# First normalisation of a two-block layer kernel in two halves of 512 tokens

## The reference, cut to what matters

```python
def rms_norm(x, w):
    xf = x.astype(jnp.float32)
    y = xf * lax.rsqrt(jnp.mean(xf * xf, axis=-1, keepdims=True) + EPS)
    return (y * w.astype(jnp.float32)).astype(x.dtype)

def hybrid_block(x, norm1_w, w_in, ...):
    h = rms_norm(x, norm1_w)
    proj = h @ w_in            # q, k, v of the attention come first here
...
def s5_ssm(u, a_re, a_im, log_dt, ...):
    lam = lax.complex(a_re, a_im)
    dt = jnp.exp(log_dt)[:, None]
    a_bar = jnp.exp(lam * dt)
    zoh = (a_bar - 1.0) / lam
```

## Time and profile before

| | |
|---|---|
| median of 3 runs | 3429.97 us (3427.22 to 3436.2) |
| profiled execution, its time | 3430.34 us |
| its span (first to last instruction) | 3428.4 us |
| mean granted TensorE clock | 0.983 |
| TensorE busy | 96% of the span |
| VectorE, ScalarE, POOL busy | 43%, 30%, 38% |
| first product pair starts | 37.26 us |
| block 2 starts | 64.49 us |

### The profile page before, as it was taken

One profiled execution on the slowest core, in us unless ns is written; L12 is line 12 of the kernel. 1 busy time (PEld: TensorE's weight loads), 2 busy tenths in 40 slices (PEclk: granted clock), 3 DMA queues, 4 the chain that ended last, 5 costly groups with the idle time before them and its releaser, 6 DMA issues. The chain is left out here.

```text
span 3428.4 us, 51094 instructions
## 1 busy us (share of the span) xinstructions
PE 3283.3 (96%) x20680; PEld 2707.5 (79%) x20680; DVE 1479.0 (43%) x2368; ACT 1012.7 (30%) x1728; POOL 1315.8 (38%) x1102
## 2 busy tenths in 40 slices
PE   6999999999898999999999999999899999999999
PEld 5888888777787887887788888888688877777877
DVE  4333333263656555457633333333382144444343
ACT  3444444432443434301211111111222044432221
POOL 4222222252424242335434333344434355554543
PEclk9999999999999999999899999999899999999999
DMA  2100000103112011214111111111331111111122
GB/s 105 36 32 32 31 32 32 38 22 112 37 32 56 20 49 28 87 54 156 51 57 49 43 49 49 49 49 49 120 87 47 48 46 42 52 46 46 58 86 80
DMA packets 104198, 188.06 MB, mean 55 GB/s; under 512 B 32328, under 2 KB 64712, under 8 KB 101328
## 3 DMA queue, kind: packets, MB, share of 16 engines
q1 hardware_dynamic: 91536, 179.19, 16.0%
q10 hardware_dynamic: 12480, 6.29, 0.6%
HBM read 158.33 MB, written 27.12 MB: 54 GB/s over the span
## 5 line engine op out<-in xcount | busy, mean ns | idle before, releaser
L303 PE MATMUL DP<-XH,WH 128*128 128x512 f32 x2592 | 832.6, 402 | 18.3 <-POOL WL L251 18.3
L249 POOL CAST WH<-WRAW 128x1024 fp32r<-128x1024 f32 (+2 forms) x258 | 269.2, 1043 | 1484.2 <-issue 900.5
L303 PE MATMUL DP<-XL,WH 128*128 128x512 f32 x2592 | 804.7, 392 | 0.0
L303 PE MATMUL DP<-XH,WL 128*128 128x512 f32 x2592 | 803.5, 391 | 0.0
L251 POOL TENSOR_TENSOR WL<-WRAW,WH 128x1024 fp32r<-128x1024 f32 (+2 forms) x258 | 588.5, 2281 | 20.8
L303 PEld LDWEIGHTS DP<-XH,WL 128*128 128x128 f32 x2592 | 488.7, 189 | 105.6
L303 PEld LDWEIGHTS DP<-XL,WH 128*128 128x128 f32 x2592 | 488.8, 189 | 105.0
L303 PEld LDWEIGHTS DP<-XH,WH 128*128 128x128 f32 x2592 | 467.6, 189 | 120.0 <-issue 24.3
L870 DVE SCALAR_TENSOR_TENSOR SS<-B,RQ,SBI 128x256 f32<-128x256 f32 (+2 forms) x192 | 74.3, 428 | 314.8 <-PE B L569 314.8
L379 DVE TENSOR_TENSOR XR<-XR,B 128x1024 f32<-128x1024 f32 x88 | 106.6, 1220 | 90.7 <-PE B L359 88.4
L2320 DVE SCALAR_TENSOR_TENSOR TG<-DP,COL,TG 128x1023 f32<-128x1023 f32 x44 | 56.4, 1283 | 199.8 <-ACT TG L2308 197.0
(11 more groups left out here) (480 smaller groups left out, 5176.3 us busy)
## 6 DMA issues: line engine op xcount, KB each, us to landing
WRAW<-in_w_up SPq DMA_DIRECT2D x44, 512.0 KB, 3.5
WRAW<-in_w_attn SPq DMA_DIRECT2D x36, 512.0 KB, 3.5
WRAW<-in_w_down SPq DMA_DIRECT2D x22, 512.0 KB, 3.5
XR<-in_x SPq DMA_DIRECT2D x8, 1024.0 KB, 8.0
WRAW<-in_w_dn SPq DMA_DIRECT2D x16, 512.0 KB, 3.8
aa_dram<-AA ACTq DMA_DIRECT2D x12, 512.0 KB, 3.3
YY<-yy_dram SPq DMA_DIRECT2D x12, 512.0 KB, 4.1
WRAW<-in_w_lrux SPq DMA_DIRECT2D x10, 512.0 KB, 3.4
```

Of the source, the lines that this page charges most:

```text
L249: pool.tensor_copy(WH[b.slot][:, 0:b.kt, :], WRAW[b.slot][:, 0:b.kt, :]).then_inc(w_hi, 1)
L303: mm = pe.matmul(DP[b.slot][:, half * H:half * H + H], w[b.slot][:, k, :], x[:, k, half * H:half * H + H], start=one, stop=end)
```

## The change

It leaves the arithmetic as it is and splits the first normalisation, its loads and its first product pair by tokens, 0 to 511 and 512 to 1023. The other three normalisations run through the same helpers, rewritten so that they take a range of tokens, and are as before.

- SP loads the first half of x in four transfers of 0.5 MB, then constants and the two weight blocks, then the second half in three transfers, which count on `mx_out`, `ks_out` and `w1_out` (later waits on these are raised by 16). SP no longer waits for `pr_sm`.
- ScalarE squares the first half, loads the table of the root (`norm_warm`), takes the first root, and then works on both halves in an order written out below. Behind both it waits for `pr_sm` and issues the two small transfers to DRAM itself, ahead of `attn_act`, which begins with `take_q`.
- VectorE does only the angle part ahead of the normalisation; the 21 chained operations and `pr_sm` come behind the last scaling of the second half.
- TensorE's `product2_halves` takes the first half for all k of both blocks, with the second half's sums ahead of k = 4 and its transposes ahead of k = 6; then the second half for k = 0 to 3 of both blocks, then k = 4 to 7 of block 0, then of block 1.
- `NTL`, `SQ`, `RS`, `XH` and `XL` keep their places; each half uses its own columns of them.

```diff
+        def scale_one(dve, c, k, src, w):
+
+            if k == 0:
+                dve.wait_ge(rs_sum, c.root + 2)
+            if k >= 2:
+                dve.wait_ge(nt_used, c.nt + k - 1)
+            elif c.nt0:
+                dve.wait_ge(nt_used, c.nt0)
+            dve.scalar_tensor_tensor(out=NTL[k % 2][:, c.tok], in0=src[:, k, c.tok], scalar=col(w, k), in1=c.spread,
+                                     op0=ALU.mult, op1=ALU.mult).then_inc(nt_ready, 1)
+        def hi_one(act, c, k):
+
+            act.wait_ge(nt_ready, c.nt + k + 1)
+            act.activation(XH[:, k, c.tok], NTL[k % 2][:, c.tok], ACT.Copy).then_inc(xh_ready, 1)
...
+        def product2_halves(pe, blocks, hi, lo, cs, within=None):
+
+            for b in blocks:
+                pe.wait_ge(w_split, b.n + 1)
+                pe.wait_ge(psum_free[b.slot], b.loads - 1)
+            for half, c in enumerate(cs):
+                t = slice(half * H, half * H + H)
+                steps = [(b, k) for k in range(KD if half == 0 else 4) for b in blocks]
+                if half:
+                    steps += [(b, k) for b in blocks for k in range(4, KD)]
+                for b, k in steps:
+                    if b is blocks[0]:
+                        if half == 0 and within:
+                            within(k)
+                        pe.wait_ge(xh_ready, c.nt + k + 1)
+                        pe.wait_ge(nt_used, c.nt + k + 1)
+                    for w, x, one, end in ((WH, hi, k == 0, False), (WH, lo, False, False), (WL, hi, False, k == KD - 1)):
+                        mm = pe.matmul(DP[b.slot][:, t], w[b.slot][:, k, :], x[:, k, t], start=one, stop=end)
+                    if half and k == KD - 1:
+                        mm.then_inc(mm_done, 1)
...
@@ SP
-                    sp.dma_start(XR[:, 2 * i:2 * i + 2, :], a["x"][:, 2 * i:2 * i + 2, :]).then_inc(mx_in[i], 16)
+                    sp.dma_start(XR[:, 2 * i:2 * i + 2, 0:H], a["x"][:, 2 * i:2 * i + 2, 0:H]).then_inc(mx_in[i], 16)
                 sp.dma_start(CON[:, :], a["cst"]).then_inc(con_in, 16)
                 sp.dma_start(COL[:, :], a["cols"]).then_inc(con_in, 16)
                 for i in range(2):
                     load(sp, Block("attn", 0, i), a["w_attn"])
+                for k, n, landed in ((0, 2, mx_out), (2, 2, ks_out), (4, 4, w1_out)):
+                    sp.dma_start(XR[:, k:k + n, H:T], a["x"][:, k:k + n, H:T]).then_inc(landed, 16)
...
@@ ScalarE, behind prep_act
+                def square1(i, k):
+                    act.wait_ge((mx_out, ks_out, w1_out, w1_out)[k // 2] if i else mx_in[k // 2], 16)
+                    norm_square(act, c1[i], k, XR[:, k, c1[i].tok])
                 for k in range(KD):
-                    act.wait_ge(mx_in[k // 2], 16)
-                    norm_square(act, c1, k, XR[:, k, :])
-                norm_sqrt(act, c1)
-                norm_hi(act, c1)
+                    square1(0, k)
+                norm_warm(act)
+                norm_sqrt(act, c1[0])
+                hi_one(act, c1[0], 0)
+                hi_one(act, c1[0], 1)
+                for k in range(5):
+                    square1(1, k)
+                for k in range(5, KD):
+                    hi_one(act, c1[0], k - 3)
+                    square1(1, k)
+                hi_one(act, c1[0], 5)
+                hi_one(act, c1[0], 6)
+                norm_sqrt(act, c1[1])
+                hi_one(act, c1[0], 7)
+                norm_hi(act, c1[1])
+                act.wait_ge(pr_sm, 1)
+                act.dma_start(r8_dram, SM[:, 8, :]).then_inc(pr_out, 16)
+                act.dma_start(sk_dram, SM[:, 13:27, :].rearrange("p r t -> p (r t)")).then_inc(pr_out, 16)
                 attn_act(act)
...
@@ VectorE
+                prep_angle(dve)
+                for k in range(1, KD):
+                    norm_add(dve, c1[0], k)
+                norm_inverse(dve, c1[0])
+                dve.wait_ge(con_in, 32)
+                def scale1(i, k):
+                    scale_one(dve, c1[i], k, XR, "norm1")
+                scale1(0, 0)
+                scale1(0, 1)
+                for k in range(1, 5):
+                    norm_add(dve, c1[1], k)
+                for k in range(5, KD):
+                    scale1(0, k - 3)
+                    norm_add(dve, c1[1], k)
+                scale1(0, 5)
+                scale1(0, 6)
+                norm_inverse(dve, c1[1])
+                for k in range(7, KD):
+                    scale1(0, k)
+                for k in range(KD):
+                    scale1(1, k)
                 prep_dve(dve)
-                for k in range(1, KD):
-                    norm_add(dve, c1, k)
-                norm_inverse(dve, c1)
-                dve.wait_ge(con_in, 32)
-                norm_scale(dve, c1, XR, "norm1")
```

More of the change, by code:

```diff
@@ L394, in program, with __init__ @@
         class NormCount:
-            def __init__(self, i):
-                self.sq, self.ss, self.nt = KD * i, i, KD * i
-                self.acc, self.root = 7 * i, 2 * i
+            def __init__(self, sq, acc, nt, root, tokens=(0, KD), sums=None, spread=None, nt0=None):
+                self.sq, self.acc, self.nt, self.root, self.ss = sq, acc, nt, root, root // 2
+                self.tiles = range(*tokens)
+                self.tok = slice(P * tokens[0], P * tokens[1])
+                self.sums = B67[:, 0:16] if sums is None else sums
+                self.spread = B45[:, self.tok] if spread is None else spread
+                self.nt0 = nt if nt0 is None else nt0
@@ L400, in norm_square, with counts @@
+        def counts(n):
+            return [n + i + 1 for i in range(KD)]
         def norm_square(act, c, k, src):
             if k >= 2:
-                act.wait_ge(sq_used, c.acc + max(k - 2, 1))
-            act.activation(SQ[k % 2][:, :], src, ACT.Square).then_inc(sq_ready, 1)
+                act.wait_ge(sq_used, c.acc[max(k - 2, 1)])
+            act.activation(SQ[k % 2][:, c.tok], src, ACT.Square).then_inc(sq_ready, 1)
         def norm_add(dve, c, k):
-            dve.wait_ge(sq_ready, c.sq + k + 1)
+            dve.wait_ge(sq_ready, c.sq[k])
@@ L408, in norm_add @@
             if k > 1:
-                dve.wait_ge(sq_used, c.acc + k - 1)
-            dve.tensor_tensor(RS[:, :], (RS if k > 1 else SQ[0])[:, :], SQ[k % 2][:, :], ALU.add).then_inc(sq_used, 1)
+                dve.wait_ge(sq_used, c.acc[k - 1])
+            dve.tensor_tensor(RS[:, c.tok], (RS if k > 1 else SQ[0])[:, c.tok], SQ[k % 2][:, c.tok], ALU.add).then_inc(
+                sq_used, 1)
         def norm_sum(pe, c):
-            pe.wait_ge(sq_used, c.acc + 7)
-            for t in range(KD):
-                mm = pe.matmul(B67[:, 2 * t:2 * t + 2], RS[:, P * t:P * t + P], ONES[:, 0:2], start=True, stop=True)
+            pe.wait_ge(sq_used, c.acc[KD - 1])
@@ L417, in norm_sum, with norm_warm, norm_sqrt @@
+            for t in c.tiles:
+                mm = pe.matmul(c.sums[:, 2 * t:2 * t + 2], RS[:, P * t:P * t + P], ONES[:, 0:2], start=True, stop=True)
             mm.then_inc(rs_sum, 1)
-        def norm_sqrt(act, c):
+        def norm_warm(act):
             act.wait_ge(con_in, 32)
             act.activation(WARM[:, :], ONES[:, 0:1], ACT.Sqrt)
+        def norm_sqrt(act, c):
             act.wait_ge(rs_sum, c.root + 1)
-            act.activation(RSS[:, :], B67[:, 0:16], ACT.Sqrt, scale=1.0 / D, bias=EPS).then_inc(rs_sqrt, 1)
+            r = slice(2 * c.tiles[0], 2 * c.tiles[-1] + 2)
+            act.activation(RSS[:, r], c.sums[:, r], ACT.Sqrt, scale=1.0 / D, bias=EPS).then_inc(rs_sqrt, 1)
@@ L652, in host, with second_norm @@
                 return hook
-            product2(pe, [att_block(0, pos) for pos in range(2)], XH, XL, norm_tiles(c1))
+            def second_norm(k):
+                if k == 4:
+                    norm_sum(pe, c1[1])
+                if k == 6:
+                    norm_turn(pe, c1[1])
+            product2_halves(pe, [att_block(0, pos) for pos in range(2)], XH, XL, c1, second_norm)
             for i in range(NIT):
@@ L1280, in mx_fill @@
         def mx_fill(sp):
-            sp.wait_ge(mx_out, 128)
+            sp.wait_ge(mx_out, 16 + 128)
             sp.wait_ge(qkv_ready, NGRP - 2)
@@ L2352, in ffn_act @@
                 if t == 0:
-                    act.wait_ge(w1_out, 32)
+                    act.wait_ge(w1_out, 16 + 32)
                     for n in range(4, 8):
@@ L2694, in prep_wo @@
                 dve.sem_inc(pr_kl, 1)
-        c1, c2, c3, c4 = (NormCount(i) for i in range(4))
+        c1 = [NormCount(counts(8 * i), counts(7 * i - 1), 8 * i, 2 * i, (4 * i, 4 * i + 4), nt0=0) for i in range(2)]
+        c2, c3, c4 = (NormCount(counts(8 * i), counts(7 * i - 1), 8 * i, 2 * i) for i in (2, 3, 4))
         with nc.Block() as block:
```

57 lines of the change are left out of this document (30 added, 27 removed).

## The result

The changed kernel took 3449.69 us (median of 4 runs, 3445.34 to 3452.34) against 3429.09 (4 runs): a ratio of 1.0057, interval 1.0042 to 1.0072. That is slower by 0.6%, where I had forecast no change (3434) and a range up to 3441. Two later sets of executions gave 3448.93 and 3446.79, so it holds. The profiled execution took 3452.34 us, beside 3430.34 before.

A forecast was written before the change was run, and what follows sets the result against it. TensorE, 96% busy, was taken as the bound, so only block 2's start counted: 66.0 + 0.9 + 2.0 = 68.9 against 64.5, +4.4 us; 3430.34 + 4.4 - 0.4 = 3434 us, range 3422 to 3441.

The forecast's parts named there:

- The walk to block 2: Start of the kernel, step by step: first product at 25.2, third weight block (block 2) at 68.9 instead of 64.49.
- The turns with POOL: Before block 2: VectorE's adds, copies and small SBUF operations each wait for POOL's whole instruction; scalings don't.
- Rival 1: S5 preparations don't wait for POOL and end at 60.8; block 2 at 63.7, -0.8 us, 3429; chance 0.15.
- rival 2: Early start carried on without turns: last XL 51.2, block 2 at 56.5, -8.0 us, 3422; chance 0.13.
- The 66.0 for the preparations: VectorE's 21 small operations after the last scaling (56.3): 4.53 us alone, 5.2 lost beside POOL, done at 66.0.
- the 0.53 between an add of 1024 and one of 512 columns: Duration difference in us, subtracted from 1.28 to put a 512-column scaling at 0.75.
- one number is wanted: From block 2 to 700 us TensorE idles 0.9 of 635.6 us, so block 2's shift moves the end equally.
- Rival 3: TensorE stays at the lower clock in the first pair: +7.7 us (3438) or +10.3 (3440); chance 0.17.
- the 2.9 us that rival 3 has for the rise: If the clock stays low to 58, block 2 starts at 71.9 and loses 2.9 us more while it rises.

The follow-up runs named there:

- filled: The changed kernel with 40 unread matmuls in TensorE's idle gap ahead of block 2; 3438.21 us, ratio 1.0028.
- held: The kernel before plus 27 chained VectorE operations that ScalarE waits for before taking block 0; 3438.3 us, ratio 1.0037.
- held and filled: The kernel before with those 27 operations and ScalarE's wait, plus 31 unread matmuls in TensorE's gap; 3431.19 us, ratio 1.001.

## Why the prediction was wrong

*The walk to block 2 was right.* Weights landed by 12.5 (11.9 forecast), sums at 17.0 (17.3), first product 24.67 (25.2), second sums at 39.1 (40.7), last XL at 56.4 (58.5; 58.1 in the third set), preparations done at 66.65 (66.0), ScalarE's QA the releaser, block 2 at 69.84 (68.9). +5.35 against +4.4; 6.5 and 7.0 in the two other profiles. The turns with POOL, the whole ground of this walk, are seen directly in the preparations' rows. Rival 1 (they slip past POOL) is shown false by the pairs of 2.4 us, and so is rival 2 (no turns) by 56.4 where it wanted 51.2.
The 66.0 for the preparations is right by luck in part: they started at 54.31 and not at 56.3, and took 12.3 us and not 9.7. The walk had four of POOL's instructions in their way and left out the next ones, SBI and the split of the block after (61.15 to 66.41). One source of the walk is named wrongly: the 0.53 between an add of 1024 and one of 512 columns can't be read from the earlier trace rows, which show adds of 1.87 and 3.18 beside POOL. An add of 1024 that runs alone takes 1.23 (at 11.72 in the kernel before), so the 0.53 itself is right, and a scaling took 0.73 to 0.75.
The rule of the Trainium skill ("SBUF — State Buffer", section "SBUF: two separate sides") names VectorE operations with two SBUF inputs or in a two-port mode as those that lock; by it the 16-column operations wait, and the trace agrees (1.52 for four of them, 2.44 for two). The TENSOR_SCALAR at 55.25, which has one array as input, took 1.21 beside POOL's XL, and 0.18 at the head of the queue (in the run with the halves only). Whether it ran in a two-port mode no row tells.

*What failed* is the sentence "So whatever the start of block 2 moves by, the end moves by: one number is wanted." The row behind it, TensorE idle for 0.9 us of 635.6, is right still: idle time behind block 2 grew by 2.2 us. But that row bounds idle time and not the speed of the work. The shift is carried one for one only if TensorE runs at the same clock. It wasn't: in the profiled execution block 2 moved by 5.35 us and the end by 22.1. I had put a gap in front of block 2, 62 to 68.9 in my own walk, without a price. The gap was 9.6 us, since the pair ended at 60.2. The runs put the price at 8.6 to 10.7 us or more for this gap (changed kernel against filled) and at some 7 for one of 7.5 (held against held and filled, a rough figure).

*Rival 3 had the right mechanism and only part of its place.* I asked what a low clock would do in the pieces of the first pair. There it came in two of the three profiles of the changed kernel (block 2 1.1 and 1.7 us later) and in the filled one (3.3 us, near the 3.2 of the rival). Behind block 2 I allowed 2.9 us for it, and only if it had been low up to 58. In the first profile the spell from 31 to 38 us cost nothing that shows (TensorE was waiting for operands for part of it, and the last XL came before my 58.5); the one from 65.5 to 79.1 cost 4.3 us, because there it is what sets the pace.
The Trainium skill ("TensorE: Matmul & The Clock Gate", section "Part 1: The HAM clock gate") says the clock falls only after an idle stretch; I cited it and did not hold it against the gap. On that gap the trace agrees (9.62 us idle, then 0.50). On the later spells it doesn't: at 750 us the clock falls with TensorE busy for 35.00 of 35.00 us.

*What is not settled* is the part behind the roots, 12.4 us in the profile. That it depends on the gap, the medians show for the changed kernel: with the gap filled the roots start at 82.4 (83.4, 85.3 and 82.1 in its three profiles) but the end comes 8.6 to 10.7 us earlier. In the kernel before it is 1.8 and 7.1, and there the executions overlap. How a gap at 65 us lengthens spells hundreds of us later is not shown. Nor is a wait or an instruction of the change found there. And the gap isn't all: the halves alone, which leave no such gap, also end 10 us late with block 2 only 4.9 late, and the changed kernel with its wait moved ends 3.2 us late with block 2 0.5 early. Both have the low spell in their pair; whether it has a price further on, no run tells.

*My chances.* I gave 0.08 to slower by over 0.3%. Both the added gap and the rise afterwards stood in my own numbers. With the 2.9 us that rival 3 has for the rise (half of the 5.74 us at the lower level), the forecast would have been 3437 and the range would have reached 3444: still short of 3449.69, for the part behind the roots stood in none of my rows.

## What to carry to other kernels

When a shift ends in a new idle stretch of the engine that bounds the kernel, price the stretch, then the clock behind it; a row that says "no idle time from here on" says nothing of the speed. Before a change of several parts is judged, ask which queue each moved wait now stands in: here an engine that frees an accumulator was made to wait for 21 small operations that nobody needed yet, and moving that one wait gave back 14 to 16 of 17 to 21 us. And price small operations of VectorE beside a busy GpSimd by GpSimd's instructions: here two that take 0.38 us took 2.44 beside a WL of 2.39.

## What the runs showed of the hardware

The kernel before has 118.5 us at the lower clock behind block 2, in a span where TensorE is 96% busy, in spells of up to 20.5 us; in 14 of its 23 spells TensorE works without a gap. What it did before them differs. Ahead of 18 of the 23 (19 of 25 in the changed kernel, behind 100 us) it was idle for at least 1 us shortly before the clock fell (I counted the last 4 us). Ahead of the one at 750 us it wasn't: in the changed kernel it works without a gap from 741.5 to 776.5 and the clock falls at 751.5. Some of its matmuls there take 8 rows instead of 128 (L738); whether that matters no run tests.

The spells come at nearly the same places of the program in every version, but not with the same length: the stage at 750 us had 6.8 us before, 17.1 in the changed kernel and 3.4 in another execution of it. This is most of what makes runs of one kernel differ (3418 to 3437 us, clock 0.980 to 0.987). The product of span and mean clock is steadier: over 28 runs of the kernel before its mean is 3368.3 with a standard deviation of 2.3 us, where the times have 4.4. For the 4 runs of the changed kernel it is 3366.5. That doesn't say that the two kernels do equal work: the changed one's profile has 11.2 us of low clock ahead of block 2, where TensorE doesn't set the pace, and half of that takes 5.6 us off its product, about what block 2 is late.
